# PEER expert weights on Trainium2: each part of the gate tensor stored by two DMA queues, from three staging places

## The reference, cut to what matters

```
a   = einsum('thkd,td->thk', u_tab[ib], xb)      # one dot product for each chosen expert
w   = gelu(a) * gb                               # gb: the softmax weights, the gates
out = einsum('thk,thkd->td', w, v_tab[ib])
```

## Time and profile before

| | |
|---|---|
| median of 3 runs | 3974.59 us (3968.96 to 3977.09) |
| profiled execution, its own time | 3983.67 us |
| its span | 3981.8 us |
| TensorE busy, share of the span | 90% |
| VectorE | 71% |
| GpSimd | 42% |
| ScalarE | 21% |
| mean granted clock of TensorE | 0.944 of full speed |
| DMA | 1263.24 MB, 317 GB/s over the span |

### The profile page before, as it was taken

One profiled execution on the slowest core, in us unless ns is written; L12 is line 12 of the kernel. 1 busy time (PEld: TensorE's weight loads), 2 busy tenths in 40 slices (PEclk: granted clock), 3 DMA queues, 4 the chain that ended last, 5 costly groups with the idle time before them and its releaser, 6 DMA issues.

```text
span 3981.8 us, 38551 instructions
## 1 busy us (share of the span) xinstructions
PE 3590.4 (90%) x12502; PEld 2153.4 (54%) x12502; DVE 2810.6 (71%) x6216; ACT 846.7 (21%) x2201; POOL 1667.1 (42%) x1410
## 2 busy tenths in 40 slices
PE   8899778999868999999997977899987899999996
PEld 2345434588767844444345543458876884444442
DVE  0238986888675696666685897688868569666668
ACT  0100421116553200000002142111655420000000
POOL 2224761521373135555530466152136313555553
PEclk9899688999989999999998968899998999999998
DMA  7876883888898989999985687388889998999995
GB/s 270 285 256 260 290 279 134 314 305 278 303 407 309 325 340 361 413 413 414 412 322 185 260 286 270 137 322 297 281 299 405 334 345 318 385 414 413 405 413 231
DMA packets 420759, 1263.24 MB, mean 317 GB/s; under 512 B 37120, under 2 KB 140288, under 8 KB 383696
## 3 DMA queue, kind: packets, MB, share of 16 engines
q0 software_dynamic: 198912, 721.61, 47.9%
q1 hardware_dynamic: 121744, 488.77, 33.0%
q10 hardware_dynamic: 99904, 50.40, 4.3%
HBM read 1173.81 MB, written 86.84 MB: 317 GB/s over the span
## 4 chain that ended last, share of the span: by engine, by line
PE 43%; DMA 27%; DVE 16%; POOL 6%; issue 4%; ACT 3%; ACTq 0%; SPq 0%; DVEq 0%
PE P L826 17%; DMA ring<-in_peer_u_dram,eidx 9%; DMA ring<-in_peer_v_dram,eidx 9%; PE P L801 7%; POOL ring L580 6%; DMA gate_d<-area 6%; DVE ring L1160 5%; PE P L854 4%; PE T L838 3%; PE O L616 2%; PE P L658 2%; DMA gate_d<-hT 2%; PE V L616 2%; DVE h L1178 1%; PE V L854 1%
## 5 line engine op out<-in xcount | busy, mean ns | idle before, releaser
L580 POOL DMA_INDIRECT ring<-in_peer_u_dram,eidx x768 | 963.3, 1254 | 1187.0 <-DVE ring L1160 662.4
L1160 DVE SCALAR_TENSOR_TENSOR ring<-ring,h 128x1024 f32<-128x1024 f32 x768 | 919.9, 1222 | 280.7 <-DMA ring<-in_peer_u_dram,eidx 237.3
L580 POOL DMA_INDIRECT ring<-in_peer_v_dram,eidx x512 | 620.2, 1211 | 870.6 <-DVE late L1178 478.8
L854 PE MATMUL P<-w_ring,area 128*128 128x512 f32 x2048 | 927.6, 596 | 42.8 <-DVE area L1334 41.4
L826 PE MATMUL P<-hT,w_ring 128*128 128x256 f32 x4096 | 924.5, 384 | 0.0
L826 PEld LDWEIGHTS P<-hT,w_ring 128*128 128x128 f32 x4096 | 779.8, 193 | 102.6
L854 PEld LDWEIGHTS P<-w_ring,area 128*128 128x128 f32 x2048 | 388.1, 191 | 545.3 <-issue 544.9
L1178 DVE SCALAR_TENSOR_TENSOR h<-ring,dots,h 128x1024 f32<-128x1024 f32 x254 | 325.9, 1283 | 157.0 <-DMA ring<-in_peer_v_dram,eidx 138.0
L1178 DVE SCALAR_TENSOR_TENSOR late<-ring,dots,late 128x1024 f32<-128x1024 f32 x254 | 325.6, 1282 | 14.7
L801 PE MATMUL P<-hT,w_ring 128*128 128x128 f32 (+1 forms) x1024 | 285.3, 440 | 3.0 <-issue 2.2
L854 PE MATMUL V<-w_ring,qT 128*128 128x512 f32 x512 | 261.5, 592 | 0.0
(11 more groups left out here) (216 smaller groups left out, 3570.8 us busy)
## 6 DMA issues: line engine op xcount, KB each, us to landing
w_ring<-in_peer_uT_dram SPq DMA_DIRECT2D x128, 1024.0 KB
w_ring<-in_peer_vB_dram SPq DMA_DIRECT2D x128, 1024.0 KB
ring<-in_w_mod_dram POOLq DMA_DIRECT2D x96, 512.0 KB, 5.8
w_ring<-in_peer_wq_dram SPq DMA_DIRECT2D x64, 512.0 KB
h<-acts_d SPq DMA_DIRECT2D x64, 512.0 KB
w_ring<-in_w_in_dram SPq DMA_DIRECT2D x48, 512.0 KB
gate_d<-area ACTq DMA_DIRECT2D x48, 512.0 KB
gate_d<-hT ACTq DMA_DIRECT2D x48, 512.0 KB
```

Of the source, the lines that this page charges most:

```text
L580: pool.indirect_dma_start(out=ring[:, b, :], out_offset=None, in_=tables["uv".index(phase)], in_offset=bass.IndirectOffsetOnAxis(ap=eidx[: ...
L854: mm = pe.matmul(bank[ACC[2 * t + half]][:, :], w, uv_ring[:, b // 2 % (WR // 2), b % 2, half * 512:(half + 1) * 512], start=b == 0, stop= ...
L1160: dve.scalar_tensor_tensor(ring[:, b, :], ring[:, b, :], 1.0, h2[:, k, :], ALU.mult, ALU.mult, accum_out=dots[:, k, row:row + 1]).then_inc ...
```

## The change

A part's half h = 0 is still issued by ScalarE; half h = 1 is issued by SyncE, in `store_gates`, after the load and the activation store of the pair that `gates_with` names: the one at which TensorE has finished the block one or two behind the part's last. The last two parts of a layer thus fall into the V loop, part 23 at i == 1, ahead of the wait for all parts. A third staging place lies in `area[:, 4096:6144]`; parts 0 to 3 use places 0 and 1 in turn, later ones places 2, 0, 1, 2, ... (place 2 holds tile 4's scores until part 3 is done). Each place has its own semaphore.

```diff
+def gates_with(i):
+    ends = [first + blocks * q // CHUNKS for _, first, blocks in CHUNK_BLOCKS
+            for q in range(SUB // QUAD - 1, CHUNKS, SUB // QUAD)]
+    return [part for part, b in enumerate(ends) if (b + 9) // 2 == i]
+
+def stage_of(part):
+    places = [part % 2 if part < 4 else (2, 0, 1)[(part - 4) % 3] for part in range(part + 1)]
+    return places[part], places[:part].count(places[part])
+
+PLACED = [[stage_of(part)[0] for part in range(SUBS)].count(place) for place in range(3)]
...
-        gate_st = [area[:, 2048:4096].rearrange("p (c n) -> p c n", c=DC), hT[:, :, 0:2 * P]]
+        gate_st = [area[:, 2048:4096].rearrange("p (c n) -> p c n", c=DC), hT[:, :, 0:2 * P],
+                   area[:, 4096:6144].rearrange("p (c n) -> p c n", c=DC)]
...
+                def store_gates(part):
+                    n, q = divmod(part, SUBS // len(V_DENSE))
+                    for last in (4 * q + 2, 4 * q + 3):
+                        job = ("g", V_DENSE[n], last)
+                        sp.wait_ge(emptied[BANK[job]], emptied_at(job, l))
+                    place, _ = stage_of(part)
+                    sp.dma_start(gate_d[l].rearrange("(c h) p s n -> h s p c n", h=2)[1, part],
+                                 gate_st[place][:, :, P:2 * P]).then_inc(gate_out[place], 16)
...
                     if i >= ACTS_LATE:
                         store_acts(i - ACTS_LATE)
+                    for part in gates_with(i):
+                        store_gates(part)
...
                     if i < ACTS_LATE:
                         store_acts(BATCHES - ACTS_LATE + i)
+                    for part in gates_with(KEYS // 2 + i):
+                        store_gates(part)
                     if i == 1:
-                        for j in range(2):
-                            sp.wait_ge(gate_out[j], (l + 1) * 32 * (SUBS // 2))
+                        for j in range(3):
+                            sp.wait_ge(gate_out[j], (l + 1) * 32 * PLACED[j])
                         load_gates(0)
...
-                        if col == 0 and s >= 2:
-                            act.wait_ge(gate_out[s % 2], 32 * (l * (SUBS // 2) + s // 2))
+                        place, before = stage_of(s)
+                        if col == 0 and before:
+                            act.wait_ge(gate_out[place], 32 * (l * PLACED[place] + before))
...
-                            for h in range(2):
-                                act.dma_start(gate_d[l].rearrange("(c h) p s n -> h s p c n", h=2)[h, s],
-                                              gate_st[s % 2][:, :, h * P:(h + 1) * P]).then_inc(gate_out[s % 2], 16)
+                            act.dma_start(gate_d[l].rearrange("(c h) p s n -> h s p c n", h=2)[0, s],
+                                          gate_st[place][:, :, 0:P]).then_inc(gate_out[place], 16)
```

More of the change, by code:

```diff
@@ L386, in build @@
         act_out = [sem(f"act_out{i}") for i in range(ACT_BUFS)]
-        gate_out = [sem(f"gate_out{i}") for i in range(2)]
+        gate_out = [sem(f"gate_out{i}") for i in range(3)]
         act_ld = [sem(f"act_ld{i}") for i in range(2)]
@@ L1046, in _ @@
                         s, col = divmod(V_DENSE.index(k) * CHUNKS + q, SUB // QUAD)
-                        if col == 0 and s >= 2:
-                            act.wait_ge(gate_out[s % 2], 32 * (l * (SUBS // 2) + s // 2))
-                        st = gate_st[s % 2].rearrange("p c (e t) -> p c e t", t=SUB)[:, :, :, col * QUAD:(col + 1) * QUAD]
+                        place, before = stage_of(s)
+                        if col == 0 and before:
+                            act.wait_ge(gate_out[place], 32 * (l * PLACED[place] + before))
+                        st = gate_st[place].rearrange("p c (e t) -> p c e t", t=SUB)[:, :, :, col * QUAD:(col + 1) * QUAD]
                         act.activation(st, ready(job)[:, :].rearrange("p (t c e) -> p c e t", t=QUAD, c=DC), ACT.Copy
```

## The result

The changed kernel takes 3928.19 us (median of 4 runs, 3925.35 to 3929.69) against 3973.28 us of the kernel before (4 runs): ratio 0.9875, 95% interval 0.9859 to 0.989. The profiled execution has a span of 3925.8 us, 56 less than the one of before; some 10 of these are due to that one, at 3983.67 us, being 10 us above the median of the 4 runs.

The account below looks back on a forecast made before the run. Full DMA engines, with small-packet stores losing to gathers, were taken to bound tile 4's stretch. 15.0 + 10.4 + 4.4 - 6.8 = 23 us off the median of 3974.59 gave 3952 us, range 3930 to 3982.

Parts of the forecast that it names:

- What bounds the kernel: U phase: `gate_d` stores are slow because DMA engines are full; queues share by packets, so small packets lose.
- Step 1: Stores of gates: with half on SyncE's queue a part takes 25 to 30 us, not 35 to 41; ScalarE's issues cost nothing.
- Step 2: Third staging place: 40 us are there for 25 to 30, so ScalarE's waits for a place go.
- Step 3: Stretch to tile 4's last chunk: at most 13.0 and 8.4 us by DMA share, corrected to 15.0 and 10.4 us won.
- the corrections: Tile 4's stretch, each layer: 5 us for `v` rows falling behind it, 3 us for a shorter 1070 to 1100 us dip.
- Step 4: Tile 1's chunks, layer 0 only: the stall from the store of 19.82 us goes, 4.4 us won.
- Step 5: Passage to V: SyncE's last half delays the gates' load, TensorE 3.4 us late, twice, 6.8 us lost.
- Step 6: SyncE's waits on ScalarE's copies, ahead of loads of `u`: they cost nothing.
- the signs that I had named as right: TensorE's waits for ScalarE under 25 us, no issue over 3 us, stretch share 1.03 or more, V's weights 2 to 5 us later.
- B: Rival: more than the bytes allow by its count, 22.8 + 18.2 + 4.4 = 45 us, 3929; chance 0.15.
- C: Rival: two queues no faster than one, a part still takes 35 to 41 us; 11.7 us won, 3963; chance 0.12.
- D: Rival: slower, loads of `u` come late behind small packets on SyncE's queue; 13 us slower, 3988; chance 0.10.

Follow-up runs that it names:

- e5: Kernel before with `gate_d` laid out so that a part is one DMA of 1024 packets of 1 KB, on ScalarE's queue: 3951.62 us, ratio 0.9931.
- e6: Changed kernel with both halves of every part issued by SyncE, none by ScalarE: 3950.60 us, ratio 0.9921.
- e7: Changed kernel with part 23 stored by ScalarE alone and the last 70 `u` rows of tile 1 gathered at half length: 3875.13 us, ratio 0.9738.
- e2: Changed kernel with the third place undone: two staging places, halves split over two queues: 3949.75 us, ratio 0.9912.
- e1: Changed kernel with the split undone: three staging places, both halves issued by ScalarE: 3966.00 us, ratio 0.996.
- e9: Kernel before, but GpSimd holds tile 0's `v` rows until tile 4's last chunk: 3972.51 us, ratio 0.9986.
- e12: The kernel before, unchanged, run once more to see its spread between executions: 3978.79 us (one run).
- e8: Changed kernel with part 23 stored by ScalarE alone and SyncE's halves issued one pair of blocks earlier: 3922.56 us, ratio 0.9853.

## Why the prediction was wrong

*What bounds the kernel* held: packets in turn explain the long stores (e5, e6, and the queues' packets in the kernel before, shown behind e6), and the work of the DMA engines sets most of the stretch after the change (e7).

*Step 1* held in its mechanism: 29.6 to 32.6 us for a part (e2) instead of my 25 to 30. That I cost ScalarE's issues at nothing was right for the changed kernel (the longest takes 0.40 us), but e1 shows that with a third place alone they would have been the bound.

*Step 2* held: next to no wait for a place is left (1.4 us in both layers).

*Step 3* is the one that failed: "13.0 us at most" and "8.4 us at most", with the corrections "I take 5" and "I take 3", made 15.0 and 10.4 us. A shrank by 34.5 and 27.4 us. Two things were wrong in it: how much faster the engines could get, and how much of their work has to be done by tile 4's last chunk.

*How much faster.* I worked out the bound from shares (0.98 and 1.00, against 1.04). The same rows have 370 and 382 GB/s against 405, and by these the bound is 226 x (1 - 370 / 405) = 19.5 and 219 x (1 - 382 / 405) = 12.4 us: a share of 0.98 stood for fewer bytes than 0.98 / 1.04 of 405 GB/s, which would be 382. The kernel after, over the same stretches:

```profile
1030.00:1221.00 191.00, 167.57 (x881) 149.42 (x880) 142.08 (x261) 114.94 (x299) 116.23 (x91) 0.95 1.04 407
2891.00:3083.00 192.00, 172.14 (x883) 152.54 (x882) 142.49 (x261) 115.42 (x299) 120.25 (x93) 0.92 1.04 406
```

At 407 and 406 GB/s the bytes of before take 20.5 and 12.9 us less, where I allowed 13.0 and 8.4 and took 3 off each for the dip of 1070 to 1100 us. That dip is gone; the row of the kernel after from 1070 us has a share of 1.04.

*How much work.* I had taken nearly all that the engines did until tile 4's last chunk as work that has to be done by then. The queues over the stretch, 1010 to 1256 us in the kernel before:

```profile
DMA packets 42544, 88.33 MB, mean 359 GB/s; under 512 B 2536, under 2 KB 25064, under 8 KB 40107
...
q0 software_dynamic: 14255, 51.91, 53.0%
q1 hardware_dynamic: 5394, 24.70, 26.9%
q10 hardware_dynamic: 22880, 11.54, 15.8%
```

and 1010 to 1221 us in the kernel after:

```profile
DMA packets 40070, 82.22 MB, mean 390 GB/s; under 512 B 2352, under 2 KB 23856, under 8 KB 37827
...
q0 software_dynamic: 13257, 48.29, 56.8%
q1 hardware_dynamic: 15359, 27.97, 35.2%
q10 hardware_dynamic: 11440, 5.77, 9.1%
```

At the same point of TensorE's work 6.1 MB less have been carried, 3.6 of them gathers (as much as seven of the eight rows fetched ahead, of which GpSimd has issued five by then) and 2.5 stores and loads. Over the shorter stretches above it is 5.9 and 5.7 MB, 14.5 and 14.1 us at 407 and 406 GB/s, where I took 5 and had counted the gathers alone. 20.5 + 14.5 is the 35 us by which the first stretch is shorter, 12.9 + 14.1 the 27 us of the second. This divides the time, and doesn't show two causes that work one without the other: e9 says that carrying less isn't enough by itself (some 6 us for 4.2 MB). Behind the stretch there was room for what was put off: B had a share of 0.89 and now has 1.00, with TensorE busy for 120.00 of 120 us. My reading, which no run tests alone, is that TensorE catches up with VectorE, and that the rows fetched ahead then fall behind its last chunk.

*Step 4*: layer 0's stall is gone (4.4 us, as said). It isn't there in every execution of the kernel before: e12 has none in layer 0 (B 122.9) and one of 2.0 us in layer 1 (124.9).

*Step 5* was right in place and kind, "I take 3.4": 3.0 and 2.7 us of waiting, and 2.9 and 1.7 more that I had left out, for V's first matmuls at a slow clock (granted clock 0.58 of full speed from 1346 to 1354 us, against 1.00 at the same place, 1382 to 1390 us, in the kernel before). *Step 6* held as the change is written (0.5 us of SyncE's waits for copies in layer 0); e8 shows the wait that it avoids. All the signs that I had named as right came, while the time fell outside the range: they test steps 1, 2 and 5, and not the size of step 3.

Of the rivals B came true in its kind, "more than the bytes allow by my count"; I had put it at 0.15. That its 3929 meets the 3928.19 measured is luck: it had 22.8 and 18.2 us for the stretch and no loss at the passage, and the profiled executions show 34.5 and 27.4 us and a loss of 10.3. C fell: from two queues a part took 29.6 to 32.6 us, from one 33.3 to 45.9. The Trainium skill's "DMA: Bandwidth & Descriptors", section "Issuing engines are not separate DMA queues", which spoke for it, holds here for the total, which stayed at some 400 to 415 GB/s in the full stretches. That several engines save only the time of issuing did not hold: a second queue gave the stream of small packets a larger share. A good part of the gain is issue time all the same, since ScalarE spent some 152 us in long issues before. D didn't come.

## What to carry to other kernels

In this kernel's full stretch a queue's share went by its packets, so look at packet sizes (packets and MB of each queue) before looking for more buffers: a store in 512-byte pieces beside 4 KB gathers starved, and either larger pieces or a second queue cured most of it. A buffer more without that mostly moved the wait, here into the issuing instruction, where it blocks a compute engine. When bounding a stretch by what the DMA engines can do, take the rate in GB/s of a stretch that is really full and not the ratio of busy shares. And count only the bytes that must have landed at its end; what is fetched ahead or stored behind can move out of it.

## What the runs showed of the hardware that I had not expected

ScalarE's DMA issue is not always short. In and just ahead of tile 4's stretch the second half took 5 to 15 us to issue for six parts of each layer in the kernel before, and 12 to 17 us for five parts of each in e1, and the engine did nothing else meanwhile. SyncE's shows the same in e6 (13.62 us). With at most one half of each part in ScalarE's queue (changed kernel, e2), or with a part in 1024 packets (e5), no issue took over 0.43 us. So the unfinished packets ahead in the queue seem to be what counts; how many of them it takes isn't shown, since the trace doesn't tell when a half lands.

The busy share of the DMA engines says less than it seems to: it was 0.98 at 344 GB/s (e7) and at 370 (the kernel before), and 1.04 at 407 (after).
